# Opening of a two-block fp32 kernel: two weight units split in alternating quarters, the third block's share moved behind the third activation tile, and TensorE given small matmuls ahead of the first product

## The chip, the cores and the metric

The kernel runs on one core of one Trainium2 chip. The metric is the device time of one launch in microseconds (us). A range of 0.2% of it, some 7 us, is about what a measurement of this kernel can tell from no change.

## What is computed

Two transformer-like blocks run one behind the other on `x` of 1024 tokens by 1024 channels, all in float32. Only the opening of the first one matters here:

```python
def hybrid_layer(x, g_pre_mix, w_in, ...):
    h = rmsnorm(x, g_pre_mix)
    proj = jnp.einsum('bld,dn->bln', h, w_in)
    ...
    (u_s5, x_conv, b_conv, c_conv, q, k, v, f_logit, gate_logits) = jnp.split(proj, offsets, axis=-1)
    y_a = s5_mixer(u_s5, a_re, a_im, log_dt, b_re, b_im, c_re, c_im, d_skip, w_glu)
    y_b = short_conv_mixer(x_conv, b_conv, c_conv, conv_w)
    y_c = forgetting_attention(q, k, v, f_logit, b_f)
```

## The kernel before

**Layout.** Activations are kept transposed, channels on the 128 partitions: `x` is 8 tiles of 128 channels by 1024 tokens. A product is made block by block. A block is 128 output channels by 1024 tokens and needs one weight unit, 128 by 1024 numbers (8 squares of 128 by 128, one for each activation tile `k`), fetched from a stream in HBM in the order of use.

**Precision.** Each factor is split in a rounded high part and the rest. A product of a weight square with half an activation tile is three matmuls with 512 columns: high by high, high by low, low by high. For weights ACT casts `w_raw` to `w_hi` and POOL subtracts to get `w_lo` (`split_unit`, L276 to L284). For activations ACT writes `act_hi` (L1067), DVE writes `act_lo` (L1068). There are two slots for weight units, so a slot's next unit is fetched when its `w_lo` is done (`fetch_unit`).

**Queues.** Each engine works through its instructions in the order in which the code writes them, and waits on semaphores. An instruction that waits holds back all behind it on its engine.

**The opening** is in `s5` (the loop over `k` from L1064). The first two blocks (`first_two`, a `TwoBlocks`) and a third one (`third(k)`, weights `hi3`, `lo3`, in the trace `n1wh`, `n1wl`) are made together, tile by tile, while `x` arrives. For each `k` the order is: `act_hi`, `act_lo`, a square of `x` on ACT (`n1s`, L1073), the sum of squares on DVE (L1075), then 12 matmuls of `first_two.tile` and 6 of `third(k)`. After the tile of `k` = 0 the third unit is cast on ACT (L1084) and split on POOL (L1085); `third(0)` stands behind the tile of `k` = 1. `first_split` splits unit 0 as a whole; unit 1 is split as a whole by `first_two.tile` at its first call. Small operations of the s5 mixer (`small`, tiles `s_tm`, 128 x 16) are woven in, three steps of the generator for each `k` from 1 to 6. `squares` and their sums give the row scale `rs`, with which the blocks are evicted at the end.

**The semaphores** that the change touches: `s_whi` counts casts of units, `s_split` counts finished splits of units, and `G` (in the order listings `gpsimd`) counts marked POOL instructions. `vector` and `scalar` are the same for DVE and ACT.

Of the kernel before, what the change touches and what calls it, by code (L numbers as in the profile page):

```python
# [9 lines left out]
P = 128  # L10
L = 1024
D = 1024
KT = D // P
# [20 lines left out]
F32 = mybir.dt.float32  # L34
# [93 lines left out]
def _build(nc, ctx, t, out):  # L128
# [22 lines left out]
    V = Lane(nc.vector, sem("vector"), 1024)  # L151
# [141 lines left out]
    def first_split():  # L293

        split_unit(0, 0, 1)
        fetch_unit(2, 0)
# [116 lines left out]
    class TwoBlocks:  # L413
# [3 lines left out]
        def __init__(self, tiles, rhs, split=False, final=False, called=False):  # L417
            self.tiles, self.rhs, self.split, self.final, self.called = tiles, rhs, split, final, called
            self.base, self.begun = used["units"], False
            self.pairs = [(used["blocks"] + o) % 2 for o in range(2)]  # L420
            self.ready = {}
            advance(2, 2)

        def tile(self, o, h, k):
# [4 lines left out]
            if not self.begun:  # L429
                self.begun = True  # L430
                if not self.split and not self.called:
                    split_unit(b + 1, 1 - slot, (b + 1) // 2 + 1, 4 if b else 1)
                if not self.final:
                    fetch_unit(b + 3, 1 - slot)
            if k == 0 and h == 0:
                nc.tensor.wait_ge(s_split, b + 3)
                nc.tensor.wait_ge(reads.sem, reads.n)
# [501 lines left out]
    def s5(first_two, first_evicts, w, stored):  # L939
# [3 lines left out]
        with ExitStack() as keep:  # L943
# [103 lines left out]
            with ExitStack() as at:  # L1047
# [17 lines left out]
                for k in range(KT):  # L1065
                    g = col("g_pre_mix", k)
                    a = A.mark(A.after(arrived[k]).activation(act_hi[:, k, :], x[:, k, :], ACT.Copy, scale=g))  # L1067
                    split = V.mark(V.after(a).scalar_tensor_tensor(act_lo[:, k, :], x[:, k, :], g,  # L1068
                                                                   act_hi[:, k, :].bitcast(F32), ALU.mult, ALU.subtract))
                    if k == 0:  # L1070
                        first_split()
# [11 lines left out]
                    if k == 0:  # L1083
# [5 lines left out]
                    if k == 1:  # L1089
                        PE.after(third_ready)  # L1090
                        third(0)
                    if k == KT - 1:
                        for h in range(2):
                            spread = half_spread(h, bank[h][:], roots[h])
                            rs_ready = A.mark(A.after(spread).copy(rs[:, halves[h]], bank[h][:]))
                    if k:
                        last = third(k)
# [929 lines left out]
    with ExitStack() as at:  # L2027
# [45 lines left out]
        first_two = TwoBlocks(KT, act_rhs)  # L2073
# [172 lines left out]
```

## Time and profile before

| | before |
|---|---|
| median of 3 runs | 3443.64 us (3442.82 to 3444.27) |
| the profiled execution, its time | 3441.3 us |
| its span in the profile | 3439.6 us |
| mean granted TensorE clock | 0.996 of full speed |
| PE / DVE / ACT / POOL busy | 98% / 38% / 27% / 27% |

The span runs from the first to the last instruction; the time of the execution has 1.7 us around it. Busy shares are shares of the span. "PE" is the matmul part of TensorE, "PEld" its weight loads, which overlap it. All times in the rows are counted from the start of the span.

### The profile page before, as it was taken

How to read it: one execution, taken by the hardware profiler on the slowest of the kernel's cores; microseconds unless marked ns; L12 is line 12 of the kernel's file. 1: busy time of each engine (PE TensorE's matmuls, PEld its weight loads, DVE VectorE, ACT ScalarE, POOL GpSimd, SP SyncE). 2: the span in 40 equal slices, each digit the busy share in tenths (PEclk: the TensorE clock that was granted, in tenths of full speed). 3: DMA queues.
4: the chain of work that ended last, by engine and by line, in shares of the span. 5: the costliest groups of instructions: out<-in, count | busy, mean ns of one | idle time of the engine just before them, and what ended most of it. 6: DMA issues, size and time to landing. Idle time of an engine off the chain costs nothing.

```text
span 3439.6 us, 40933 instructions
## 1 busy us (share of the span) xinstructions
PE 3358.9 (98%) x16184; PEld 2736.7 (80%) x16184; DVE 1312.0 (38%) x1631; ACT 944.6 (27%) x1248; POOL 944.5 (27%) x507
## 2 busy tenths in 40 slices
PE   8999999999999999999999999999999999999997
PEld 6788888777877888888867777777788788888886
DVE  7852455434234131313153427555461521121123
ACT  3213444444232111111133432312352411111112
POOL 2212222213432222222321124232264222222125
PEclk9999999999999999999999999999999999999998
DMA  3535444235412111111234223214362211111113
GB/s 130 160 95 160 132 152 149 96 110 188 149 56 73 49 49 49 43 54 43 98 120 124 96 89 114 74 68 149 135 220 98 85 45 54 43 49 50 48 55 129
DMA packets 101603, 333.43 MB, mean 97 GB/s; under 512 B 11920, under 2 KB 21520, under 8 KB 101328
## 3 DMA queue, kind: packets, MB, share of 16 engines
q1 hardware_dynamic: 100432, 327.95, 28.4%
q10 hardware_dynamic: 1040, 3.67, 0.3%
q8 instruction: 90, 1.47, 0.2%
q14 instruction: 41, 0.34, 0.0%
HBM read 249.06 MB, written 85.52 MB: 97 GB/s over the span
## 4 chain that ended last, share of the span: by engine, by line
PE 86%; DVE 7%; issue 2%; DMA 2%; ACT 2%; POOL 1%; SPq 0%; DVEq 0%; ACTq 0%; POOLq 0%
PE pair L322 73%; PE pair L441 4%; PE wide L832 2%; PE bank L652 2%; PE bank L800 1%; DMA m2g<-proj 1%; PE wide L565 1%; DVE act_lo L555 1%; DVE s_tmp L958 1%; DVE hg_t L1500 1%; POOL w_lo L282 0%; DVE p L623 0%; DVE hg_pt L1519 0%; PE bank L495 0%; PE bank L473 0%
## 5 line engine op out<-in xcount | busy, mean ns | idle before, releaser
L282 POOL TENSOR_TENSOR w_lo<-w_raw,w_hi 128x1024 fp32r<-128x1024 f32 (+1 forms) x304 | 699.4, 2304 | 2337.2 <-ACT w_hi L278 2288.4
L322 PE MATMUL pair<-act_hi,w_hi 128*128 128x512 f32 x2976 | 942.0, 398 | 2.2 <-DVE p L2045 1.2
L322 PE MATMUL pair<-act_lo,w_hi 128*128 128x512 f32 x2976 | 920.0, 390 | 0.0
L322 PE MATMUL pair<-act_hi,w_lo 128*128 128x512 f32 x2976 | 918.7, 390 | 0.0
L322 PEld LDWEIGHTS pair<-act_lo,w_hi 128*128 128x128 f32 x2976 | 559.2, 188 | 119.3
L322 PEld LDWEIGHTS pair<-act_hi,w_lo 128*128 128x128 f32 x2976 | 558.9, 188 | 119.5
L322 PEld LDWEIGHTS pair<-act_hi,w_hi 128*128 128x128 f32 x2976 | 539.7, 188 | 107.0 <-issue 8.2
L278 ACT CAST w_hi<-w_raw 128x1024 fp32r<-128x1024 f32 x274 | 287.4, 1049 | 836.9 <-PE pair L322 801.0
L623 DVE TENSOR_TENSOR p<-pair,rs 128x1024 f32<-128x1024 f32 x100 | 122.2, 1222 | 403.9 <-PE pair L322 403.8
L1960 DVE TENSOR_TENSOR f2v<-pair,rs 128x1024 f32<-128x1024 f32 x42 | 51.4, 1224 | 330.7 <-PE pair L322 330.7
L322 PE MATMUL pair<-f1hh,w_lo 128*128 128x512 f32 x480 | 147.8, 389 | 0.0
L322 PE MATMUL pair<-f1hh,w_hi 128*128 128x512 f32 x480 | 147.8, 389 | 0.0
L322 PE MATMUL pair<-f1hl,w_hi 128*128 128x512 f32 x480 | 147.7, 389 | 0.0
L441 PE MATMUL pair<-act_hi,w_hi 128*128 128x512 f32 x192 | 86.4, 450 | 24.9 <-DVE act_lo L555 13.0
L1954 DVE TENSOR_TENSOR f1v<-pair,rs 128x1024 f32<-128x1024 f32 x30 | 36.7, 1225 | 183.7 <-PE pair L322 183.7
L1949 ACT CAST f1hh<-f1v 128x1024 f32 x30 | 31.5, 1050 | 273.6 <-DVE f1v L1955 273.6
L322 PEld LDWEIGHTS pair<-f1hh,w_hi 128*128 128x128 f32 x480 | 90.1, 188 | 18.7
L322 PEld LDWEIGHTS pair<-f1hh,w_lo 128*128 128x128 f32 x480 | 90.1, 188 | 18.7
L322 PEld LDWEIGHTS pair<-f1hl,w_hi 128*128 128x128 f32 x480 | 90.1, 188 | 18.7
L1986 DVE TENSOR_TENSOR f1y<-f1y,pair 128x1024 f32 x22 | 26.9, 1221 | 201.3 <-PE pair L322 201.3
L322 PE MATMUL pair<-f2hh,w_lo 128*128 128x512 f32 x328 | 101.0, 389 | 0.0
L322 PE MATMUL pair<-f2hh,w_hi 128*128 128x512 f32 x328 | 101.0, 389 | 0.0
(492 smaller groups left out, 4038.5 us busy)
## 6 DMA issues: line engine op xcount, KB each, us to landing
w_raw<-in_stream SPq DMA_DIRECT2D x275, 512.0 KB, 3.5
proj<-p SPq DMA_DIRECT2D x101, 512.0 KB, 2.6
m2g<-proj SPq DMA_DIRECT2D x32, 512.0 KB, 5.8
m1g<-proj SPq DMA_DIRECT2D x16, 512.0 KB, 3.6
x<-f1y SPq DMA_DIRECT2D x16, 512.0 KB, 2.6
act_lo<-x SPq DMA_DIRECT2D x16, 512.0 KB, 6.9
foxx<-proj SPq DMA_DIRECT2D x28, 256.0 KB, 5.8
fx_cb<-fox_cum SPq DMA_DIRECT2D x8, 512.0 KB, 7.3
```

What stands on the lines that cost most here:

```text
L278: nc.scalar.copy(whi[:, slot, :], raw[:, slot, :]).then_inc(s_whi, 1)
L282: last = nc.gpsimd.tensor_tensor(wlo[:, slot, at:at + n], raw[:, slot, at:at + n], whi[:, slot, at:at + n].bitcast(F32), ALU.subtract)
L322: last = nc.tensor.matmul(out_pair[:, h * HALF:(h + 1) * HALF], wt, a[:, h * HALF:(h + 1) * HALF], start=k == 0 and n_pass == 0, stop=k == ...
L441: last = nc.tensor.matmul(out, wt, a[:, half], start=k == 0 and n_pass == 0, stop=k == self.tiles - 1 and n_pass == 2)
L555: split[h, k] = V.mark(V.after(a).scalar_tensor_tensor(act_lo[:, k, half], yk, g, act_hi[:, k, half].bitcast(F32), ALU.mult, ALU.subtract))
L565: done[h].append(PE.mark(nc.tensor.matmul(sides[h], ones[:], sq(h, k % 2), start=k == 0, stop=k == KT - 1)))
L623: done = read(V.after(ready, stored).tensor_tensor(buf[:, slot, :], psum[:], rs[:], ALU.mult))
L652: last = nc.tensor.transpose(dst_j, src(j0 + j), ident[:])
L800: last = nc.tensor.matmul(bank[1][mine, n % 4 * P:(n % 4 + 1) * P], vt[:, k0 // P + j, mine], p[:, j, :], start=j == 0, stop=j == nk - 1)
L832: last = nc.tensor.matmul(wide[:, c:e], q[:, h % 2, q0:q0 + P], ks[:, h % 2, k0 + c:k0 + e], start=q is qh, stop=q is ql)
L1954: a = read(V.then(ready).tensor_tensor(x[:, s, :], psum[:], rs[:], ALU.mult))
L1960: v = read(V.then(ready).tensor_tensor(x[:, o, :], psum[:], rs[:], ALU.mult))
```

## The change

Four things are done. (1) `first_split` casts both first units one behind the other and subtracts them in eight pieces of 256 columns, by turns, each with its own mark; `first_two.tile` waits for the piece that it needs instead of a whole unit, and doesn't split unit 1 itself. (2) ACT and DVE make the second activation tile (`scaled(1)`) directly behind the two casts, ahead of both squares and of the third unit's cast. (3) The third unit's cast and split stand behind the tile of `k` = 1, and `third(0)` and `third(1)` stand behind the tile of `k` = 2. (4) TensorE gets 14 matmuls of `ones` by `ones`, 128 x 128 in float32, as soon as `ones` is written; their output in `bank[1]` is used by nobody.

```diff
--- before.py
+++ after.py
@@ -290,9 +290,21 @@
 
     for n in range(2):
         fetch_unit(n, n)
-    def first_split():
-
-        split_unit(0, 0, 1)
+    def first_split(pieces):
+
+        for b in range(2):
+            nc.scalar.wait_ge(s_raw[b], 16)
+            nc.scalar.wait_ge(s_mm, b + 1)
+            nc.scalar.copy(whi[:, b, :], raw[:, b, :]).then_inc(s_whi, 1)
+        for b, n in ((0, 0), (0, 1), (1, 0), (0, 2), (1, 1), (0, 3), (1, 2), (1, 3)):
+            if n == 0:
+                nc.gpsimd.wait_ge(s_whi, b + 3)
+            two = slice(2 * n * P, 2 * (n + 1) * P)
+            low = nc.gpsimd.tensor_tensor(wlo[:, b, two], raw[:, b, two], whi[:, b, two].bitcast(F32), ALU.subtract)
+            if n < 3:
+                pieces[b, 2 * n] = G.mark(low)
+            else:
+                low.then_inc(s_split, 1)
         fetch_unit(2, 0)
 
     def products(i, base, per_turn, n_out, tiles, rhs, evict, ahead=False):
@@ -414,8 +426,9 @@
 
 
 
-        def __init__(self, tiles, rhs, split=False, final=False, called=False):
+        def __init__(self, tiles, rhs, split=False, final=False, called=False, pieces=None):
             self.tiles, self.rhs, self.split, self.final, self.called = tiles, rhs, split, final, called
+            self.pieces = pieces
             self.base, self.begun = used["units"], False
             self.pairs = [(used["blocks"] + o) % 2 for o in range(2)]
             self.ready = {}
@@ -428,12 +441,15 @@
             reads, out = pair_read[self.pairs[o]], pair[self.pairs[o]][:, half]
             if not self.begun:
                 self.begun = True
-                if not self.split and not self.called:
+                if not self.split and not self.called and self.pieces is None:
                     split_unit(b + 1, 1 - slot, (b + 1) // 2 + 1, 4 if b else 1)
                 if not self.final:
                     fetch_unit(b + 3, 1 - slot)
+            if self.pieces and h == 0:
+                PE.after(self.pieces.get((b, k)))
+            if h == 0 and k == (KT - 2 if self.pieces else 0):
+                nc.tensor.wait_ge(s_split, b + 3)
             if k == 0 and h == 0:
-                nc.tensor.wait_ge(s_split, b + 3)
                 nc.tensor.wait_ge(reads.sem, reads.n)
             hi, lo = self.rhs(o, k)
             w_hi, w_lo = (x[:, slot, k * P:(k + 1) * P] for x in (whi, wlo))
@@ -1062,13 +1078,23 @@
                                                     start=k == 0 and n_pass == 0, stop=k == KT - 1 and n_pass == 2)
                     return last
 
-                for k in range(KT):
+                def scaled(k):
+
                     g = col("g_pre_mix", k)
                     a = A.mark(A.after(arrived[k]).activation(act_hi[:, k, :], x[:, k, :], ACT.Copy, scale=g))
-                    split = V.mark(V.after(a).scalar_tensor_tensor(act_lo[:, k, :], x[:, k, :], g,
-                                                                   act_hi[:, k, :].bitcast(F32), ALU.mult, ALU.subtract))
+                    return V.mark(V.after(a).scalar_tensor_tensor(act_lo[:, k, :], x[:, k, :], g,
+                                                                  act_hi[:, k, :].bitcast(F32), ALU.mult, ALU.subtract))
+
+                PE.after(ones_ready)
+                for _ in range(14):
+                    nc.tensor.matmul(bank[1][:, 0:P], ones[:], ones[:], start=True, stop=True)
+                for k in range(KT):
                     if k == 0:
-                        first_split()
+                        split = scaled(0)
+                        first_split(first_two.pieces)
+                        second = scaled(1)
+                    else:
+                        split = scaled(k) if k > 1 else second
                     sq_k = sq[:, 1 + k % 2, :] if k else squares
                     a = A.mark(A.after(added.get(k - 2)).activation(sq_k, x[:, k, :], ACT.Square))
                     if k:
@@ -1080,20 +1106,21 @@
                     for o in range(2):
                         for h in range(2):
                             first_two.tile(o, h, k)
-                    if k == 0:
+                    if k == 1:
                         a = A.mark(A.after(raw3_in).copy(hi3[:], raw3[:]))
                         third_ready = G.mark(G.after(a).tensor_tensor(lo3[:], raw3[:], hi3[:].bitcast(F32), ALU.subtract))
                         for n in range(3):
                             s5_in.mark(SP.dma_start((bb[:, 0:2, :, :], cc[:], dg[:])[n], (t["s5_b"], t["s5_c"], t["s5_d"])[n]))
                         got = s5_in.last()
-                    if k == 1:
+                    if k == 2:
                         PE.after(third_ready)
                         third(0)
+                        third(1)
                     if k == KT - 1:
                         for h in range(2):
                             spread = half_spread(h, bank[h][:], roots[h])
                             rs_ready = A.mark(A.after(spread).copy(rs[:, halves[h]], bank[h][:]))
-                    if k:
+                    if k > 1:
                         last = third(k)
                     if 0 < k < KT - 1:
                         for _ in range(3):
@@ -2070,7 +2097,7 @@
             SP.wait_ge(*v)
             return store.mark(SP.dma_start(s5_u.rearrange("(n p) j m -> n p (j m)", p=P)[1], staged))
 
-        first_two = TwoBlocks(KT, act_rhs)
+        first_two = TwoBlocks(KT, act_rhs, pieces={})
         with Woven(products(0, used["units"], n, n, KT, act_rhs, evict), n * KT, 1) as w:
             s5(first_two, (evict_row, evict_u_half, evict_third), w, stored)
             w.upto(14 * KT + 1)
```

Lines of the changed kernel have other numbers: L441 becomes L457, L1061 L1077, L1067 L1084, L1068 L1085, L1073 L1099, L1075 L1101, L1084 L1110, L1085 L1111, L958 L974, L962 L978, L966 L982, L963 L979.

**POOL, the weight splits of the opening.** In the kernel before, from `ones` on (`w_lo` are the units 0, 1 and then 2, `n1wl` is the third block's):

```order
L261 MEMSET ones 128x128 [waits gpsimd]
L282 TENSOR_TENSOR w_lo<-w_raw,w_hi 128x1024 [waits whi] x2
L1085 TENSOR_TENSOR n1wl<-n1wr,n1wh 128x1024 [waits scalar]
L282 TENSOR_TENSOR w_lo<-w_raw,w_hi 128x256 [waits whi]
L282 TENSOR_TENSOR w_lo<-w_raw,w_hi 128x256 x3
```

In the changed kernel, the same stretch:

```order
L261 MEMSET ones 128x128 [waits gpsimd]
L303 TENSOR_TENSOR w_lo<-w_raw,w_hi 128x256 [waits whi]
L303 TENSOR_TENSOR w_lo<-w_raw,w_hi 128x256
L303 TENSOR_TENSOR w_lo<-w_raw,w_hi 128x256 [waits whi]
L303 TENSOR_TENSOR w_lo<-w_raw,w_hi 128x256 x5
L1111 TENSOR_TENSOR n1wl<-n1wr,n1wh 128x1024 [waits scalar]
```

Two subtractions of 1024 columns have become eight of 256; the third unit's is still one of 1024, and still behind them.

**ACT, from the first activation tile to the third.** Before (`s_tm` are the small operations of the s5 mixer):

```order
L1067 ACTIVATE act_hi<-n1x,vec 128x1024 [waits load]
L278 CAST w_hi<-w_raw 128x1024 [waits mm,raw0]
L1073 ACTIVATE n1s<-n1x 128x1024
L278 CAST w_hi<-w_raw 128x1024 [waits mm,raw1]
L1084 CAST n1wh<-n1wr 128x1024 [waits store]
L1067 ACTIVATE act_hi<-n1x,vec 128x1024 [waits x_in1]
L1073 ACTIVATE n1s<-n1x 128x1024
L987 ACTIVATE s_tm<-vec 128x16 [waits vector]
L990 ACTIVATE s_tm<-s_tm 128x16 [waits vector]
L991 ACTIVATE s_tm<-s_tm 128x16 [waits scalar]
L1067 ACTIVATE act_hi<-n1x,vec 128x1024 [waits x_in2]
```

After:

```order
L1084 ACTIVATE act_hi<-n1x,vec 128x1024 [waits load]
L298 CAST w_hi<-w_raw 128x1024 [waits mm,raw0]
L298 CAST w_hi<-w_raw 128x1024 [waits mm,raw1]
L1084 ACTIVATE act_hi<-n1x,vec 128x1024 [waits x_in1]
L1099 ACTIVATE n1s<-n1x 128x1024 x2
L1110 CAST n1wh<-n1wr 128x1024 [waits store]
L1003 ACTIVATE s_tm<-vec 128x16 [waits vector]
L1006 ACTIVATE s_tm<-s_tm 128x16 [waits vector]
L1007 ACTIVATE s_tm<-s_tm 128x16 [waits scalar]
L1084 ACTIVATE act_hi<-n1x,vec 128x1024 [waits x_in2]
```

The second `act_hi` has moved ahead of the first square and of `n1wh`; the third `act_hi` still stands behind all of them. DVE's own order is the same in both kernels: two `act_lo`, the first sum, nine small operations, the third `act_lo`.

**PE, from the end of the tile of `k` = 1 to that of `k` = 2.** Before (`pair` are the first two blocks, `wide` is the third; twelve `wide` matmuls stand in a row):

```order
L441 MATMUL pair<-act_hi,w_lo 128x512
L1061 MATMUL wide<-act_hi,n1wh 128x512 [waits gpsimd]
L1061 MATMUL wide<-act_lo,n1wh 128x512
L1061 MATMUL wide<-act_hi,n1wl 128x512
...
L441 MATMUL pair<-act_hi,w_hi 128x512 [waits vector]
```

After:

```order
L457 MATMUL pair<-act_hi,w_lo 128x512
L457 MATMUL pair<-act_hi,w_hi 128x512 [waits gpsimd,vector]
...
L457 MATMUL pair<-act_hi,w_lo 128x512
L1077 MATMUL wide<-act_hi,n1wh 128x512 [waits gpsimd]
...
L457 MATMUL pair<-act_hi,w_hi 128x512 [waits vector]
```

The twelve `wide` matmuls that stood between the tiles of `k` = 1 and `k` = 2 now stand behind the latter, with the six of `third(2)`.

## Rows read from the trace of the kernel before

**Rows 1.** The page: shares of the chain that ended last.
```profile
PE 86%; DVE 7%; issue 2%; DMA 2%; ACT 2%; POOL 1%; SPq 0%; DVEq 0%; ACTq 0%; POOLq 0%
```

**Rows 2.** Timeline of PE: start us, us, instruction [idle before <-releaser].
```profile
11.00 0.77 PE L441 MATMUL pair<-act_hi,w_hi 128*128 128x512 f32 x1 [11.00 <-POOL w_lo L282]
...
13.70 0.63 PE L441 MATMUL pair<-act_hi,w_hi 128*128 128x512 f32 x1
...
16.56 0.50 PE L441 MATMUL pair<-act_hi,w_hi 128*128 128x512 f32 x1 [0.86 <-DVE act_lo L1068]
...
22.13 0.39 PE L441 MATMUL pair<-act_hi,w_hi 128*128 128x512 f32 x1
...
26.21 0.46 PE L441 MATMUL pair<-act_hi,w_hi 128*128 128x512 f32 x1
```

**Rows 3.** Timeline of ACT, the start.
```profile
8.94 1.03 ACT L278 CAST w_hi<-w_raw 128x1024 fp32r<-128x1024 f32 x1
...
12.26 1.15 ACT L1067 ACTIVATE act_hi<-n1x,vec 128x1024 fp32r<-128x1024 f32 x1
13.31 1.04 ACT L1073 ACTIVATE n1s<-n1x 128x1024 f32<-128x1024 f32 x1
...
18.83 1.13 ACT L1067 ACTIVATE act_hi<-n1x,vec 128x1024 fp32r<-128x1024 f32 x1
```

**Rows 4.** Timeline of DVE, the start.
```profile
7.25 1.28 DVE L1068 SCALAR_TENSOR_TENSOR act_lo<-n1x,vec,act_hi 128x1024 fp32r<-128x1024 f32 x1 [7.25 <-ACT act_hi L1067]
13.44 3.06 DVE L1068 SCALAR_TENSOR_TENSOR act_lo<-n1x,vec,act_hi 128x1024 fp32r<-128x1024 f32 x1 [4.90 <-ACT act_hi L1067]
16.54 1.22 DVE L1075 TENSOR_TENSOR n1s<-n1s 128x1024 f32<-128x1024 f32 x1
17.79 0.17 DVE L962 TENSOR_SCALAR s_tm<-vec 128x16 f32<-128x16 f32 x1
...
19.30 0.60 DVE L966 SCALAR_TENSOR_TENSOR s_tm<-s_tm 128x16 f32<-128x16 f32 x3
...
20.01 1.28 DVE L1068 SCALAR_TENSOR_TENSOR act_lo<-n1x,vec,act_hi 128x1024 fp32r<-128x1024 f32 x1
```

**Rows 5.** Timeline of POOL, the start.
```profile
2.38 0.20 POOL L261 MEMSET ones<- 128x128 f32 x1
8.16 4.92 POOL L282 TENSOR_TENSOR w_lo<-w_raw,w_hi 128x1024 fp32r<-128x1024 f32 x2 [5.58 <-ACT w_hi L278]
13.05 2.37 POOL L1085 TENSOR_TENSOR n1wl<-n1wr,n1wh 128x1024 fp32r<-128x1024 f32 x1
47.19 2.80 POOL L282 TENSOR_TENSOR w_lo<-w_raw,w_hi 128x256 fp32r<-128x256 f32 x4 [31.78 <-ACT w_hi L278]
```

**Rows 6.** Timelines of POOL and DVE from 1004: four quarters beside DVE work.
```profile
1004.49 4.10 POOL L282 TENSOR_TENSOR w_lo<-w_raw,w_hi 128x256 fp32r<-128x256 f32 x4 [1.39 <-ACT w_hi L278]
...
1004.96 1.22 DVE L555 SCALAR_TENSOR_TENSOR act_lo<-f1y,vec,act_hi 128x512 fp32r<-128x512 f32 x1
```

**Rows 7.** Timeline at 226: a small DVE operation beside POOL.
```profile
226.25 2.38 POOL L282 TENSOR_TENSOR w_lo<-w_raw,w_hi 128x1024 fp32r<-128x1024 f32 x1 [12.24 <-ACT w_hi L278]
226.41 2.31 DVE L639 TENSOR_TENSOR s_tmp<-s_tmp 128x64 f32<-128x64 f32 x1
```

**Rows 8.** DMA issues under way from 1.7 to 1.8 us, last: us to landing.
```profile
n1x<-in_x ACTq DMA_DIRECT2D x1, 512.0 KB, 6.7
w_raw<-in_stream SPq DMA_DIRECT2D x1, 512.0 KB, 7.1
```

**Rows 9.** Busy us of PE, PEld, DVE, ACT, POOL by stretch; then PEclk, DMA, GB/s.
```profile
1809.30:1812.70 3.40, 0.06 (x1) 0.00 (x0) 2.35 (x2) 3.38 (x4) 0.85 (x1) 1.00 0.03 11
...
1813.50:1816.90 3.40, 3.40 (x10) 2.66 (x9) 3.40 (x3) 0.00 (x0) 1.53 (x1) 0.50 0.00 0
```

**Rows 10.** Timeline of PE at 88 us, after a shorter idle time.
```profile
88.28 0.66 PE L652 MATMUL bank<-ident,s_state 128*128 128x128 f32 x4 [2.65 <-DVE s_state L958]
```

**Rows 11.** The chain that ended last, 0 to 110 us: two half_spread calls.
```profile
47.35 1.80 PE bank L495 x16
```

## The prediction

> **What bounds the kernel now.** I read the page first: 86% of the chain that ended last are matmuls of PE [rows 1]. Time is gained or lost here only by making PE start or stop at another moment, and the change touches only the opening. So the rest was read as a block that moves as a whole. Then I read the timelines of the four engines there. On PE [rows 2] the reader is to see three things. The first matmul waits for `w_lo` until 11.00. The first six take until 13.70, 0.45 us each, where the 18 from 22.13 to 26.21 take 4.08, 0.227 each: a slow beginning. And PE sits idle once, 0.86 us before 16.56, for the second `act_lo`. From 16.56 to 26.21 there are 42 matmuls at 0.23, so nothing more is lost. From 26.21 on (`k` = 3) the same matmuls remain in both kernels. **The question is only when `k` = 3 can start.**
>
> On DVE [rows 4] the second `act_lo` took 3.06 us, a later one 1.28. It was asked for at 13.44, while POOL's `n1wl` ran from 13.05 to 15.42 [rows 5], and ended 1.08 us behind that. At 226 us even an operation with 64 columns took 2.31 us, for as long as POOL was at a split of 1024 columns [rows 7]. DVE does not start on two SBUF inputs while POOL subtracts. I take this as the rule of the sum: the one that comes second waits for the other's whole instruction. The Trainium skill says the same ("SBUF — State Buffer", SBUF: two separate sides): the port pair that both share is an exclusive lock held for the whole instruction, not a split of bandwidth. It speaks against this change, which puts more DVE work into POOL's busy stretch; both rows of it agree, with 3.06 and 2.31 us. Without the rule the sum would be that of rival 1 (3441.9), with it the one below.
>
> **The start of PE.** Quarter (0,0) can start at 8.16 as before [rows 5]. The first `act_lo` holds DVE until 8.53 [rows 4]; four quarters alone take 2.80, 0.70 each [rows 5], so the piece ends about 9.1. Before, the whole first split ended near 13.08 - 2.37 = 10.7 (8.16 + 4.92 = 13.08 for both, 2.37 for one alone) and PE started 0.3 later. PE now starts at about 9.4, 1.6 earlier.
>
> **The 14 small matmuls.** Two `half_spread` calls, 8 float32 matmuls of this shape, take 1.80 us [rows 11], 0.225 each; at half the clock 0.45. They start when `ones` is done (2.58) and last 3.2 to 6.3 us, to 5.8 to 8.9. That ends before 9.4, so they delay nothing. If they bring the clock up, the first 12 matmuls take 0.23 instead of 0.43 to 0.45. The Trainium skill ("TensorE: Matmul & The Clock Gate", Why this matters for your kernels) tells to keep TensorE busy and to warm it up. By that rule, 1.7 us less at the front (8 cold matmuls at 0.2) would be 1.7 less in all, and with the 1.6 of the earlier start 3443.6 - 3.3 = 3440.3. From the rows I count nothing for either, since the next two waits cover both.
>
> **The wait for the second tile.** The second `w_raw`, issued at 1.7 to 1.8, lands 7.1 later [rows 8], so its cast stays near 8.85 to 9.9 [rows 3]. The second `x` tile has landed by then (at most 1.8 + 6.7 = 8.5), and the third, next on its queue, some 2.5 later. The second `act_hi` follows the cast, 9.8 to 10.95 (1.15 long, before 12.26 to 13.41). POOL is meanwhile at (1,0) from 9.95, (0,2) from 10.65 to 11.35. DVE waits for that piece and ends 1.1 later: `act_lo` is ready at 12.45, four us earlier than 16.50. PE has finished `k` = 0 by 12.3 (the block-1 half of it waits for (1,0), 10.95) and works on `k` = 1 from 12.5 to 15.2, or to 17.6 if its clock is low.
>
> **The wait for the third tile, where the gain goes.** ACT goes on with two squares (1.04 each) and the third unit's cast, 10.85 to 13.8. POOL and DVE take turns. Rows for this: beside DVE work four quarters took 4.10 instead of 2.80, and a 512-wide DVE operation 1.22 [rows 6]. In turns: (1,1) ends 13.0; the sum of squares asked at 12.85 (1.22 long) ends 14.05; (0,3) ends 14.65; the small chain starts at 14.1 instead of 17.79. Before, the third `act_hi` began 18.83 - 17.79 = 1.04 after it [rows 3, 4]; now 15.15, ended 16.3. (1,2) ends 15.35, (1,3) 16.05. Then `n1wl`, whose cast has long been done, takes POOL from 16.0 to 18.4. DVE has three small two-input operations left at that moment (0.60 for three), and behind them the third `act_lo`, which has its input from 16.3 on. They wait until 18.4, then 0.5 for the small ones, 0.2 for the one behind, 1.28 for `act_lo`: it ends at **20.35**, against 20.01 + 1.28 = 21.29 before. So it is only 0.9 earlier.
>
> Before, PE had the 12 matmuls of `third(0)` and `third(1)` to do during this wait, and reached `k` = 2 at 22.13 without a pause. Now they stand behind `k` = 2. PE is done at 15.2, idle for some 5 us, and begins `k` = 2 at 20.4. Then come 12 + 18 matmuls before `k` = 3: 30 x 0.227 = 6.8, so `k` = 3 starts at 27.2 instead of 26.21, **1.0 us later**. DVE's fourth `act_lo` ended before 26.21, at most 4.9 behind the third; now it is there by 25.3 and not the bound.
>
> **The clock behind that pause.** Behind a stretch of 3.40 us in which PE was busy for 0.06, the granted clock was 0.50 (1.2 GHz) from 1813.50 to 1816.90, with 10 matmuls in 3.40 us [rows 9]. After 2.65 us idle at 88.28 [rows 10] it was not seen to fall. Five us is past both. While the clock is at half, each matmul costs 0.2 more. A stretch like that of rows 9 overlaps the 30 matmuls wholly (8 matmuls, 1.6 us) or in part, or two in a row (up to 3.2). Bounds 0 and 3.2; I take 1.6, since the pause is longer than the one in the row.
>
> **What is hidden.** The fetches of units 2 and 3 are issued some 3 us later, since `s_split` counts whole units; all `x` tiles are queued ahead of them, and the s5 constants behind them on SP are used long after. The longer POOL stretch ends by 18.4 and its next work is at 47.19 [rows 5]. The sum of squares, the roots and the evictions follow PE.
>
> **Sum.** +1.0 + 1.6 = +2.6 us. The profiled execution (3441.3 us, 1.7 above its span) would be 3443.9; the runs shown have their median 2.3 above that execution, so 3443.64 + 2.6 = **3446.2**, which is no change by the 0.2% (6.9 us) that a measurement here can tell.
>
> **Rivals.**
> 1. *`n1wl` does not get in before the third `act_lo`* (pieces slower, or small operations not held up). Against it: it needs DVE to be some 0.9 us ahead of my turns, since `act_lo` could start at 16.95 at best and `n1wl` is due at 16.0. Then `act_lo` ends at 18.2 or earlier and `k` = 2 starts 2.1 us sooner: 27.2 - 2.1 = 25.1, a gain of 1.1; the pause is 3 us and may leave the clock up. Time 3442.5. If DVE and POOL didn't hinder each other at all, 17.6 and 3441.9. The end of this line is PE without any pause, `k` = 2 at 15.2: 22.0, 3439.4.
> 2. *The pause comes, but the clock stays.* +1.0: 3444.6. Against it rows 9; it is the lower part of my own case.
> 3. *Slower by over 0.2%.* One mechanism: the clock stays at half for longer after the pause. Each matmul costs 0.2, so beyond the +1.0 it takes 5.9 / 0.2 = 30 matmuls, all those up to `k` = 3, to decide it. Against it: in rows 9 it was 0.50 for 3.4 us while PE was fed without a break, as it would be here. With 35 it would be 3451.6.
> 4. *The small matmuls don't raise the clock,* or it falls again before 9.4. Then `k` = 0 ends near 14.5 and `k` = 1 near 17.6 to 19.6, still before 20.35: no change of the forecast, though in rival 1 it would take back up to its gain.
>
> **How the numbers follow.** My case, `k` = 3 between 26.3 and 31 (rival 2 in it): 0.78, its own range 3443.8 to 3448.5. Rival 1: 0.15. Rival 3: 0.04. 0.03 is left for a gain over 6.9 us, for which the opening has no room (PE starting at 9.4 without a pause gives 4.2) and which would have to come from elsewhere. The range takes in most of rival 1 and the two bounds of the clock: 3441.0 to 3449.0. Within 0.2% falls all but rival 3 and the rest: faster 0.03, same 0.93, slower 0.04.
>
> **What would show it.** In the changed trace: first product at 9.4; the second `act_lo` ending near 12.5 with POOL's pieces around it; `k` = 2 preceded by an idle time of PE of 4 to 5.5 us, released by `act_lo` L1085; that `act_lo` ending 1.9 to 2.2 us behind `n1wl`; the granted clock at 0.50 soon after 18; `k` = 3 at 28.8, give or take 1.5. I am wrong if the third `act_lo` runs before `n1wl`, if DVE's small operations run beside POOL, or if some stretch far behind the opening changes by more than a us on its own.

## The result and the profile after

| | before | changed |
|---|---|---|
| median, 20 runs each | 3443.57 us (3439.87 to 3447.74) | 3448.41 us (3445.38 to 3451.88) |
| ratio changed / before, 95% interval | | 1.0014 [1.0008, 1.0020] |
| profiled execution: time / span | 3441.3 / 3439.6 us | 3446.68 / 3445.0 us |
| mean granted TensorE clock | 0.996 | 0.994 |

The changed kernel is 4.8 us slower, 0.14%: less than the 0.2% that was called no change, but its interval leaves out 1. The profiled executions stand 5.4 us apart. The mean clocks are to be read with care: in the kernel before PEclk stands at 1.00 from 11.0 to 14.6, though the matmuls there come every 0.43 us, so the slow start is not in its mean.

PE's timeline of the changed kernel, to be laid beside [rows 2]:

```profile
2.74 5.62 PE L1090 MATMUL bank<-ones 128*128 128x128 f32 x28 [2.74 <-POOL ones L261]
9.31 0.47 PE L457 MATMUL pair<-act_hi,w_hi 128*128 128x512 f32 x1 [0.96 <-DVE act_lo L1085]
...
12.50 0.50 PE L457 MATMUL pair<-act_hi,w_hi 128*128 128x512 f32 x1
...
15.13 0.39 PE L457 MATMUL pair<-act_hi,w_lo 128*128 128x512 f32 x1
20.95 0.79 PE L457 MATMUL pair<-act_hi,w_hi 128*128 128x512 f32 x1 [5.43 <-DVE act_lo L1085]
21.54 0.63 PE L457 MATMUL pair<-act_lo,w_hi 128*128 128x512 f32 x1
...
24.53 0.41 PE L457 MATMUL pair<-act_hi,w_lo 128*128 128x512 f32 x1
24.77 0.40 PE L457 MATMUL pair<-act_hi,w_hi 128*128 128x512 f32 x1
...
29.54 0.39 PE L457 MATMUL pair<-act_hi,w_hi 128*128 128x512 f32 x1
```

The first product starts at 9.31 instead of 11.00, `k` = 1 at 12.50 instead of 16.56. All of that is gone at the next step. PE is done with `k` = 1 at 15.5 and then idle for 5.43 us, until the third `act_lo`. The twelve `wide` matmuls that filled this time before stand behind. And where `k` = 2 begins, matmuls come every 0.43 us; from 24.53 on every 0.23. `k` = 3 starts at 29.54 instead of 26.21: **3.3 us late.**

The same moment on POOL and DVE, beside [rows 4, 5], and ACT, beside [rows 3]:

```profile
8.24 7.86 POOL L303 TENSOR_TENSOR w_lo<-w_raw,w_hi 128x256 fp32r<-128x256 f32 x8 [5.65 <-ACT w_hi L298]
16.07 2.34 POOL L1111 TENSOR_TENSOR n1wl<-n1wr,n1wh 128x1024 fp32r<-128x1024 f32 x1
```

```profile
10.94 1.51 DVE L1085 SCALAR_TENSOR_TENSOR act_lo<-n1x,vec,act_hi 128x1024 fp32r<-128x1024 f32 x1 [2.32 <-ACT act_hi L1084]
12.91 1.23 DVE L1101 TENSOR_TENSOR n1s<-n1s 128x1024 f32<-128x1024 f32 x1 [0.46 <-ACT n1s L1099]
14.17 0.59 DVE L978 TENSOR_SCALAR s_tm<-vec 128x16 f32<-128x16 f32 x1
15.04 0.42 DVE L974 TENSOR_TENSOR s_tm<-s_tm 128x16 f32<-128x16 f32 x1 [0.28 <-ACT s_tm L1003]
15.50 0.65 DVE L974 TENSOR_TENSOR s_tm<-vec,s_tm 128x16 f32<-128x16 f32 x1
16.18 2.69 DVE L978 TENSOR_SCALAR s_tm<-s_tm 128x16 f32<-128x16 f32 x3
18.90 0.59 DVE L982 SCALAR_TENSOR_TENSOR s_tm<-s_tm 128x16 f32<-128x16 f32 x3
19.53 0.17 DVE L979 TENSOR_SCALAR s_tm<-s_tm 128x16 f32<-128x16 f32 x1
19.62 1.28 DVE L1085 SCALAR_TENSOR_TENSOR act_lo<-n1x,vec,act_hi 128x1024 fp32r<-128x1024 f32 x1
```

```profile
8.81 1.05 ACT L298 CAST w_hi<-w_raw 128x1024 fp32r<-128x1024 f32 x1 [0.65 <-DMA w_raw<-in_stream]
9.76 1.15 ACT L1084 ACTIVATE act_hi<-n1x,vec 128x1024 fp32r<-128x1024 f32 x1
...
15.87 1.13 ACT L1084 ACTIVATE act_hi<-n1x,vec 128x1024 fp32r<-128x1024 f32 x1
```

The reader is to see who holds whom. The second `act_lo` is 1.51 long instead of 3.06 and ends at 12.45: the part of the change that does what it says. The sum of squares behind it gets its turn at once (1.23) and it is a POOL piece that waits. The three small operations behind that wait for the POOL piece in progress; one of 16 columns takes 0.42 to 0.65. At 16.07 `n1wl` takes POOL until 18.41. The three `TENSOR_SCALAR` that start at 16.18 last 2.69 together, because the first is held for all of `n1wl` (three of them took 0.59 at 18.67 in the trace before). The third `act_hi` has been there since 17.0. Its `act_lo` stands in DVE's queue behind seven small operations and starts at 19.62, to end at 20.90.

The busy time by stretches (columns: length; busy of PE, PEld, DVE, ACT, POOL; PEclk; DMA share; GB/s):

```profile
15.50:17.70 2.20, 0.02 (x1) 0.00 (x0) 2.17 (x2) 2.17 (x4) 2.20 (x2) 1.00 1.02 417
17.71:20.94 3.23, 0.00 (x0) 0.00 (x0) 2.99 (x9) 1.52 (x2) 0.71 (x1) 0.50 0.92 335
20.95:24.53 3.58, 3.58 (x9) 2.81 (x10) 2.61 (x10) 2.07 (x5) 0.00 (x0) 0.50 0.03 13
24.54:29.50 4.96, 4.96 (x23) 4.13 (x22) 4.79 (x7) 4.96 (x6) 0.00 (x0) 1.00 0.01 3
...
92.81:99.63 6.82, 6.05 (x21) 4.59 (x20) 6.79 (x4) 2.10 (x3) 4.53 (x1) 0.50 0.30 97
```

The granted clock is 0.50 (1.2 GHz) from 17.7 to 24.5, that is over the second half of the pause and the first eight matmuls of `k` = 2. A second low stretch of 6.8 us lies at 92.8, 1.3 us behind a pause of 2.67 that the kernel before has too [rows 10]. Follow one matmul through it, first in the changed kernel, then in the kernel before:

```profile
91.50 0.66 PE L668 MATMUL bank<-ident,s_state 128*128 128x128 f32 x4 [2.67 <-DVE s_state L974]
...
102.57 0.63 PE L668 MATMUL bank<-ident,s_state 128*128 128x128 f32 x4 [0.77 <-ACT s_first L672]
```

```profile
96.58 0.63 PE L652 MATMUL bank<-ident,s_state 128*128 128x128 f32 x4 [0.77 <-ACT s_first L656]
```

The pause at 88 us ends 3.22 us later than before (91.50 against 88.28). At the matmul behind the low stretch it is 5.99 (102.57 against 96.58). Near the end it is 5.4:

```profile
3429.93 2.08 PE L511 MATMUL bank<-ident,tok 128*128 128x128 f32 x8 [4.13 <-DVE tok L509]
```

Before, this one stands at 3424.54. So the 5.4 us of the profiles are 3.2 from the opening, 2.8 from the clock at 92.8, and -0.6 over the rest. In the opening, 1.5 us are the order (20.95 + 30 x 0.227 = 27.76 against 26.21) and 1.8 the clock (29.54 - 27.76). At full clock e2, below, took 6.98 for these 30 matmuls, since the first of them is longer; counted so, it is 1.7 and 1.6.

### The profile page after: what moved, and what is told of

It reads as the page before. It is cut to its first block, busy times and chain, and to the rows that moved or that the text cites. A ratio compares the mean times of both kernels' runs of the same rounds, so it can differ in the third digit from the quotient of the medians.

```text
span 3445.0 us, 40998 instructions
## 1 busy us (share of the span) xinstructions
PE 3366.4 (98%) x16212; PEld 2744.2 (80%) x16212; DVE 1313.7 (38%) x1631; ACT 945.1 (27%) x1248; POOL 946.8 (27%) x513
## 3 DMA queue, kind: packets, MB, share of 16 engines
q1 hardware_dynamic: 100432, 327.95, 28.4%
## 4 chain that ended last, share of the span: by engine, by line
PE 88%; DVE 7%; issue 2%; ACT 1%; DMA 1%; POOL 0%; SPq 0%; DVEq 0%; ACTq 0%; POOLq 0%
PE pair L334 75%; PE pair L457 4%; PE wide L848 2%; PE bank L668 2%; PE bank L816 1%; PE wide L581 1%; DVE act_lo L571 1%; DVE s_tmp L974 1%; DVE hg_t L1527 1%; DVE p L639 0%; DVE hg_pt L1546 0%; PE bank L511 0%; PE bank L489 0%; DVE f1y L555 0%; DVE s_state L974 0%
## 5 line engine op out<-in xcount | busy, mean ns | idle before, releaser
L457 PE MATMUL pair<-act_hi,w_hi 128*128 128x512 f32 x192 | 86.3, 450 | 19.7 <-DVE act_lo L571 13.1
```

Source lines behind the costliest of these rows:

```text
L457: last = nc.tensor.matmul(out, wt, a[:, half], start=k == 0 and n_pass == 0, stop=k == self.tiles - 1 and n_pass == 2)
```

## The experiments

Medians of 11 runs; each group has its own runs of the kernel before beside it. The intervals of the ratios are about 0.0009 to each side, 3 us. So **the opening is read from the profiles, the medians only bear it out**. Where the first products start also differs by some 0.5 us between executions of like programs, with the landing of the first tiles.

| run | first product | `k` = 2 | `k` = 3 | `k` = 4 | median | before beside it |
|---|---|---|---|---|---|---|
| before | 11.00 | 22.13 | 26.21 | 30.39 | | 3443.57 |
| changed | 9.31 | 20.95 | 29.54 | 33.62 | 3448.41 | 3443.57 |
| e1_no_small | 9.86 | 22.27 | 32.08 | 36.16 | 3445.89 | 3443.51 |
| e2_filled_pause | 9.38 | 21.91 | 28.89 | 32.97 | 3447.17 | 3443.51 |
| e3_third_behind | 9.69 | 19.21 | 27.75 | 31.82 | 3445.75 | 3443.51 |
| e4_n1wl_quarters | 9.39 | 21.39 | 29.81 | 33.89 | 3448.78 | 3443.51 |
| e8_thirds_ahead | 9.49 | 23.93 | 28.48 | 32.56 | 3445.54 | 3442.58 |
| e5_small_alone | 11.11 | 22.42 | 26.50 | 30.64 | 3445.81 | 3442.58 |
| e6_chain_behind | 9.77 | 16.36 | 19.71 | 28.83 | 3442.52 | 3442.58 |
| e7_before_again | 11.12 | 22.26 | 26.34 | 30.51 | 3440.97 (one) | 3442.58 |
| e9_best_no_small | 9.46 | 17.24 | 19.96 | 28.63 | 3440.64 | 3443.82 |
| e12_best_small | 9.27 | 16.12 | 19.49 | 28.58 | 3441.99 | 3443.82 |
| e10_small_again | 11.49 | 22.77 | 26.85 | 31.05 | 3444.92 | 3443.82 |
| e11_change_again | 9.29 | 21.92 | 30.50 | 34.58 | 3450.76 | 3443.82 |

(`k` = 4 is comparable in all rows: the same 72 matmuls lie ahead of it everywhere.)

**e1_no_small: without the small matmuls.**

```diff
-                PE.after(ones_ready)
-                for _ in range(14):
-                    nc.tensor.matmul(bank[1][:, 0:P], ones[:], ones[:], start=True, stop=True)
```

> The changed kernel without its 14 small matmuls. Account A (the opening's delay comes from the third activation tile waiting behind n1wl, with PE in a pause): the first product at 9.3, the first twelve matmuls at 0.43 to 0.45 us each, k = 1 done before 18; k = 2 still starts at 20.9 +- 0.3, since its act_lo comes no earlier; time within 1.5 us of the changed kernel (3448.4). Account B (the small matmuls themselves, or the clock that they raise early, cause the loss or set when the clock falls later): k = 2 starts elsewhere, or the time goes back by 2 to 5 us towards 3443.6.

The first products were slow as expected and `k` = 1 was over at 17.9. `k` = 2 came at 22.27, not 20.95, since the whole chain ran later in this execution (the second weight unit landed later, its cast began at 10.11 instead of 8.81, and the second `act_lo` ended at 13.74, 1.3 later). The third `act_lo` ended 8.48 behind the second, in the changed kernel 8.45: the small matmuls have no part in the wait. The clock was low from 21.6 to 28.4, that is over nearly all the first matmuls of `k` = 2, so the 30 matmuls took 9.81 us, 2.8 more than at full clock. This profiled execution was the slowest of its 11 (3450.58). The median is 2.5 us under the changed kernel, outside the 1.5 that account A allowed and inside account B's 2 to 5, although the opening is no shorter; it comes up again below.

**e2_filled_pause: 22 matmuls more, into the pause.**

```diff
                     if k == 1:
+                        for _ in range(22):
+                            nc.tensor.matmul(bank[1][:, 0:P], ones[:], ones[:], start=True, stop=True)
                         a = A.mark(A.after(raw3_in).copy(hi3[:], raw3[:]))
```

> The changed kernel with 22 more small matmuls behind the tile of k = 1 (about 5 us of work that nobody uses, into the pause). Account A: k = 2 starts at 20.9 as before, the granted clock stays 1.00 there, and k = 3 starts at 20.9 + 30 x 0.227 = 27.7 instead of 29.5; time 1.8 us (1.6 to 2.6) under the changed kernel, 3446.6, still 1.5 to 3 over before. Account B (the clock has nothing to do with the pause): half the clock near 18 to 24 all the same, k = 3 at 29.5, time as the changed kernel.

Its PE timeline:

```profile
21.91 0.50 PE L457 MATMUL pair<-act_hi,w_hi 128*128 128x512 f32 x1 [0.53 <-DVE act_lo L1085]
...
28.89 0.39 PE L457 MATMUL pair<-act_hi,w_hi 128*128 128x512 f32 x1
```

From `k` = 2 to `k` = 3 it took 6.98 us instead of 8.59, 30 matmuls at 0.23, with the granted clock at 1.00 throughout. So the clock behind the pause costs 1.6 us, and the pause is its cause. The other profiles bear that out: in all six with a pause of 2.93 us or more before the third tile (changed, e1, e3, e4, e8, e11) the clock fell in it or within 0.4 us behind it, in none of the four where PE waited 0.53 us or less there (e2, e6, e9, e12). `k` = 3 came at 28.89 and not at 27.7, since `k` = 2 came 1.0 later here (the second unit's cast began at 9.76). The median is 1.2 us under the changed kernel, less than the 1.6 to 2.6 expected, which intervals of 3 us can't tell apart.

**e3_third_behind: the third unit's cast and split behind the third `act_lo`.**

```diff
-                    if k == 1:
+                    if k == 2:
                         a = A.mark(A.after(raw3_in).copy(hi3[:], raw3[:]))
-                        third_ready = G.mark(G.after(a).tensor_tensor(lo3[:], raw3[:], hi3[:].bitcast(F32), ALU.subtract))
+                        third_ready = G.mark(G.after(a, split).tensor_tensor(lo3[:], raw3[:], hi3[:].bitcast(F32), ALU.subtract))
+                    if k == 1:
```

> The changed kernel with the third unit's cast and split moved behind the act_lo of k = 2, nothing else. Account A: POOL is free from 16.1, the nine small DVE operations end by 17.1, act_lo of k = 2 ends at 18.3 instead of 20.9, k = 2 starts at 18.4, n1wl ends at 21.5 and third(0) waits some 0.3 us for it; k = 3 starts at 25.5 to 26 if the clock stays (pause 3.0 us), up to 27.5 if it falls; time 3442.9 to 3445, clearly under the changed kernel. Account B (DVE isn't held by the lock but by its own chain of small operations with ACT): act_lo of k = 2 still ends at 20 or later, time as the changed kernel.

The third `act_lo` now ends 6.34 us behind the second instead of 8.45, at 19.16. So `n1wl`'s place ahead of it cost 2.1 us. `k` = 3 stands at 27.75, just past the upper end: the pause was 3.32, the clock was low for a part of `k` = 2, and `k` = 2 itself came 0.8 later than expected. The median, 3445.75, missed its range (3442.9 to 3445) too.

**e4_n1wl_quarters: `n1wl` in four pieces.**

```diff
-                        third_ready = G.mark(G.after(a).tensor_tensor(lo3[:], raw3[:], hi3[:].bitcast(F32), ALU.subtract))
+                        G.after(a)
+                        for q in range(4):
+                            two = slice(2 * q * P, 2 * (q + 1) * P)
+                            low = nc.gpsimd.tensor_tensor(lo3[:, two], raw3[:, two], hi3[:, two].bitcast(F32), ALU.subtract)
+                        third_ready = G.mark(low)
```

> The changed kernel with n1wl made in four pieces of 256 columns, nothing else. Account A (exclusive, held for one instruction at a time): DVE's operations get in between the pieces; the first small one waits 0.6 us instead of 2.2, act_lo of k = 2 ends at 19.3 to 19.9 instead of 20.9, n1wl ends 1 to 2 us later than 18.4, k = 2 starts at 19.4 to 20; time 1 to 2 us under the changed kernel. If POOL keeps the lock over its pieces: act_lo at 20.9, time as the changed kernel.

The turns were as account A says, the times were not: it had the third `act_lo` at 19.3 to 19.9 and a gain of 1 to 2 us. POOL, then DVE in this stretch:

```profile
16.73 2.76 POOL L1114 TENSOR_TENSOR n1wl<-n1wr,n1wh 128x256 fp32r<-128x256 f32 x4
```

```profile
16.83 2.02 DVE L978 TENSOR_SCALAR s_tm<-s_tm 128x16 f32<-128x16 f32 x3
18.88 1.06 DVE L982 SCALAR_TENSOR_TENSOR s_tm<-s_tm 128x16 f32<-128x16 f32 x3
...
20.06 1.28 DVE L1085 SCALAR_TENSOR_TENSOR act_lo<-n1x,vec,act_hi 128x1024 fp32r<-128x1024 f32 x1
```

DVE does get in between the pieces, so the lock is held for one instruction. But each small operation buys only itself that place and the next one waits for the next quarter: three took 2.02 us, 0.65 each. Four of the seven small ones paid for a quarter, which is as long as one wait for the whole. The third `act_lo` ended 8.24 behind the second (at 21.34), 0.2 better than with `n1wl` whole, and the median stayed at the changed kernel's.

**e8_thirds_ahead: `third(0)` and `third(1)` in front of `k` = 2 again.**

```diff
-                    if k == 2:
+                    if k == 1:
                         PE.after(third_ready)
                         third(0)
-                        third(1)
...
-                    if k > 1:
+                    if k:
                         last = third(k)
```

> The changed kernel with third(0) and third(1) ahead of the tile of k = 2 again, as in the kernel before. Account A: PE pauses from 15.4 to n1wl's end, about 18.7, does the twelve matmuls until 21.4 and goes on with k = 2 at once; k = 3 at 25.5 if the clock stays, up to 27.3 if it falls in the pause of 3.2 us; 2 to 4 us under the changed kernel, -1 to +1 against the kernel before. If the moved matmuls aren't what made the pause dear, it stays near the changed kernel (k = 3 at 29).

```profile
18.64 0.80 PE L1077 MATMUL wide<-act_hi,n1wh 128*128 128x512 f32 x1 [2.93 <-POOL n1wl L1111]
...
23.93 0.63 PE L457 MATMUL pair<-act_hi,w_hi 128*128 128x512 f32 x1
...
28.48 0.39 PE L457 MATMUL pair<-act_hi,w_hi 128*128 128x512 f32 x1
```

`third(0)` starts behind `n1wl`, after 2.93 us idle, and the twelve matmuls run while `act_lo` is made: `k` = 3 comes 1.1 earlier than in the changed kernel (28.48). It missed the expected 25.5 to 27.3, since the clock was low from 18.0 to 24.9 and `third(0)`, `third(1)` took 5.3 us instead of 2.7. The pause is 2.50 us shorter than in the changed kernel (2.93 against 5.43), the 30 matmuls behind it took 1.25 longer (9.84 against 8.59), because more of them fell into the low clock, and this execution began 0.18 later: that leaves the 1.1. The median is 2.9 us under the changed kernel, as expected, but 3.0 over the kernel before, where -1 to +1 was expected.

**e5_small_alone and e10_small_again: the kernel before with the 14 small matmuls.**

```diff
+                PE.after(ones_ready)
+                for _ in range(14):
+                    nc.tensor.matmul(bank[1][:, 0:P], ones[:], ones[:], start=True, stop=True)
                 for k in range(KT):
                     g = col("g_pre_mix", k)
```

> The kernel before with the 14 small matmuls alone. Account A (they win nothing, since the second act_lo is waited for anyway): the first product at 11.0 as before, the first twelve matmuls at 0.23 us instead of 0.43, k = 1 at 16.6 and k = 3 at 26.2 as before, time within 1 us of the kernel before. By the page's rule (the clock won at the front passes through): 1.7 us under it.

> The kernel before with the 14 small matmuls alone, a second time. Account A (its 3.2 us over the kernel before in the first comparison were chance: low stretches of the clock that fall where they fall): median within 1.5 us of the kernel before, k = 3 at 26.2 to 26.5. Account C (they cost something systematic): again 2 to 3.5 us over it.

Two stretches of the first one, columns as above:

```profile
11.20:14.50 3.30, 3.30 (x8) 2.62 (x9) 0.68 (x1) 2.81 (x3) 3.30 (x2) 0.50 1.03 420
...
89.70:96.40 6.70, 5.93 (x19) 4.39 (x18) 6.67 (x4) 2.24 (x4) 4.54 (x1) 0.50 0.25 101
```

In the opening both did as the kernel before (`k` = 3 at 26.50 and 26.85, each 15.4 us behind its first product, before 15.2). But the first matmuls were not faster: the small ones end at 8.5, 2.64 us ahead of the first product at 11.1, and the granted clock was 0.50 from there to 14.5 (in the second one to 17.1). A warm-up that ended 2.64 and 3.42 us early won nothing. The low stretch at 89.7 is also here, in a kernel whose work there is unchanged.

The medians were 3.2 and 1.1 us over the kernel before. Two more pairs differ in the small matmuls alone: changed against e1_no_small (+2.5) and e12_best_small against e9_best_no_small (+1.35). The signs agree, and no single ratio to the kernel before stands out of its interval. Taken by means and together they do: the four differences of the means are 2.7, 2.0, 2.1 and 1.6, with standard errors of 0.7 to 0.9, and their average is 2.1 with one of 0.4. (The changed kernel and e1 come from two comparisons.)

The profiles show where such a time would lie. It is not in the opening, it is in stretches of low clock behind it:

| low clock between `k` = 4 and 3410 us, in all | executions | from `k` = 4 to the end of the span |
|---|---|---|
| about 10 us | before, e7, e9 | 3408.4 to 3409.2 us |
| about 14 us | e2, e3, e6 | 3411.7 to 3412.0 us |
| about 17 us | changed, e8 | 3411.4 and 3412.9 us |
| about 20 us | e1, e4, e5, e10, e11, e12 | 3412.2 to 3415.8 us |

All ten executions with small matmuls ahead stand in the lower three rows; of the four without them three are in the first row and one, e1, is in the last. If the small matmuls had no part in it, the three shortest would all be executions without them about once in 90 times (4 of 364). The comparison was made after the fact, with one execution for most kernels, and no run shows how matmuls that end before 9 us could bring low stretches hundreds of us later. It is likely, not shown.

**e7_before_again and e11_change_again: both kernels unchanged.**

> The kernel before, unchanged, one look for a second profile of it. Account A: k = 3 starts at 26.2 give or take 0.5; the granted clock may fall at other places than in the first profile (at 92 us behind the pause of 2.65, at 799), since the same program shows its low stretches at places that differ from execution to execution.

> The changed kernel, unchanged, again. Account A: k = 3 at 28.5 to 31, depending on where the low stretch lies in the pause; 3 to 4 us over the kernel before from the opening, the rest of the first comparison's 4.8 chance: median 2.5 to 5 over it. If the stretch 84 to 100 us of the first profile (18.7 us instead of 15.9) belongs to the change, it is there again.

The kernel before gave the same opening, without a low stretch near 92. The changed kernel showed `k` = 3 at 30.50 (the second `act_lo` ended 1.0 later than in the first profile) with the clock low from 18.6 to 25.4 and again from 93.7 to 100.5. Its median is 6.9 us over the kernel before, where 2.5 to 5 was expected; the profiled execution was the slowest of its 11. Over 14 profiles of all these kernels, the pause of 2.65 to 2.69 us near 88 was followed by a low stretch in nine, not in the two of the kernel before, e1, e2 and e3. Near 800, where the code is the same too, nine of the 14 had one.

**e6_chain_behind, then e9 and e12: what stood ahead of the third `act_lo` moved away.**

```diff
-                    if k == 1:
+                    if k == 3:
                         a = A.mark(A.after(raw3_in).copy(hi3[:], raw3[:]))
-                        third_ready = G.mark(G.after(a).tensor_tensor(lo3[:], raw3[:], hi3[:].bitcast(F32), ALU.subtract))
+                        third_ready = G.mark(G.after(a, split).tensor_tensor(lo3[:], raw3[:], hi3[:].bitcast(F32), ALU.subtract))
+                    if k == 1:
...
-                    if k == 2:
+                    if k == 3:
                         PE.after(third_ready)
-                        third(0)
-                        third(1)
+                        for j in range(3):
+                            third(j)
...
-                    if k > 1:
+                    if k > 2:
                         last = third(k)
-                    if 0 < k < KT - 1:
-                        for _ in range(3):
+                    if 2 < k < KT - 1:
+                        for _ in range(5 if k < 5 else 4):
```

> The changed kernel with both things that stood ahead of the third act_lo moved: the s5 mixer's small operations begin only behind the tile of k = 3 (5, 5, 4, 4 steps), and the third unit's cast and split stand behind the act_lo of k = 3, with third(0) to third(3) behind that tile. Account A: act_lo of k = 2 ends at 16.5 (with the eight pieces by turns), k = 2 starts at 16.6 with a pause of 1.0 us, k = 3 behind it without one, third(0) at about 22.2, k = 4 at 27.6 to 28.5 instead of 30.4 before and 33.6 in the changed kernel; clock 1.00 throughout; time 2 to 3 us under the kernel before, 3441. If something else holds PE up in the opening, k = 4 starts at 30 or later.

> The run with both moved behind the tile of k = 3, without the 14 small matmuls, and with 3, 5, 5, 5 steps of the s5 mixer's small operations at k = 3 to 6 (they held the act_lo of k = 4 up to 28.7). Account A (only the opening differs, and the small matmuls are neutral there, because k = 4 waits for n1wl and act_lo): k = 4 at 28.4 to 29 instead of 30.4 before; time 1.5 to 2 us under the kernel before. Account C (small matmuls ahead of the first product cost some 2 us somewhere far behind the opening): this kernel is 2 us or more under the same with them.

> The same with the 14 small matmuls. Account A: as without them, within 1 us; k = 4 at 28.6. Account C: 2 us more than without them, level with the kernel before.

e9 and e12 have `range(3 if k == 3 else 5)` in the last line, and e9 no small matmuls. PE's timeline of e9:

```profile
9.46 0.76 PE L457 MATMUL pair<-act_hi,w_hi 128*128 128x512 f32 x1 [9.46 <-POOL w_lo L303]
...
14.48 0.40 PE L457 MATMUL pair<-act_hi,w_hi 128*128 128x512 f32 x1
...
17.24 0.39 PE L457 MATMUL pair<-act_hi,w_hi 128*128 128x512 f32 x1
...
19.96 0.39 PE L457 MATMUL pair<-act_hi,w_hi 128*128 128x512 f32 x1
...
23.01 0.50 PE L1077 MATMUL wide<-act_hi,n1wh 128*128 128x512 f32 x1 [0.17 <-POOL n1wl L1108]
...
28.63 0.39 PE L457 MATMUL pair<-act_hi,w_hi 128*128 128x512 f32 x1
```

The first twelve matmuls are slow (0.42 each; this kernel leaves the small matmuls out). From 14.48 on the tiles follow one another without a pause over 0.4 us, the clock stays up, and `k` = 4 starts at 28.63: 1.8 us ahead of the kernel before and 5.0 ahead of the changed one. e6 and e12 show the same at 28.83 and 28.58. In e6 the third `act_lo` ends 3.37 us behind the second, against 6.34 in e3 and 8.45 in the changed kernel: of the 5.1 us that stood ahead of it the small operations with their turns were 3.0, `n1wl` 2.1.

The medians follow only in part. e6's, 3442.52, is level with the kernel before beside it (3442.58), though 2 to 3 us less was expected, and its `k` = 4 lies a little past the expected 27.6 to 28.5. e12's is 1.8 us under the kernel before and 1.35 over e9's; account A had allowed 1 us between the two, account C had asked for 2. e9's median, 3440.64, is the lowest of all: 3.2 under the kernel before (0.9994 [0.9985, 1.0003]) and 7.8 under the changed one. Against the changed kernel that is clear; against the kernel before the opening is shown, the time only likely.

## Why the prediction held, point by point

- **Start of PE** (predicted 9.4): 9.31. **Second `act_lo`** (12.45): 12.45. **The pieces by turns** ending at 16.05 with `n1wl` to 18.4: 16.1 and 18.41. The last two rest on one rule, that DVE and POOL take turns by whole instructions. It held in the opening of every run.
- **Third `act_lo`** (20.35): 20.90. I had taken `TENSOR_SCALAR`, which has one SBUF input, to pass beside POOL. It does not: 16 columns took 0.59 at 14.17 and the first of the three at 16.18 waited for all of `n1wl`. So the chain ahead of `act_hi` took 0.7 more than counted: 0.4 by that first operation, and 0.2 by the `TENSOR_TENSOR` at 15.04 (0.42 instead of 0.18), which has two inputs and which my own rule would have held up; I had left its turn out. Seven small operations were left behind `n1wl` instead of four. Only this cost anything, 0.55 us: `act_hi` was ready at 17.0, well before its `act_lo` could start. The Trainium skill ("SBUF — State Buffer", SBUF: two separate sides) names DVE operations in a 2-port mode beside those with two inputs as contending. The rows here agree with that and not with my narrower use of it; in which mode this `TENSOR_SCALAR` ran, no trace here shows.
- **The pause and the order term** (5 us idle, `k` = 3 later by 1.0): 5.43 idle, and 1.5. The step that was too small is the one above.
- **The clock term** (1.6, bounds 0 and 3.2): 1.6 to 1.8 in the profile, and 1.6 by filling the pause (e2). That the middle of the bounds came out is luck in part: where more of the low stretch lay over the matmuls, in e1 and e8, the 30 matmuls took 2.8 and 2.9 us more than at full clock.
- **Opening in all** (+2.6, `k` = 3 at 28.8): +3.3, 29.54. Right in its mechanism, short by 0.7.
- **The rest as a block that moves as a whole**: this part was wrong of the profiles, by the prediction's own sign (a stretch far behind the opening that changes by more than a us on its own). Another 2.8 us came from a low clock at 92.8, and the median of 20 runs moved by 4.8, 1.5 more than the opening. The cause is open. The work there is unchanged and the low stretch comes and goes with the execution, which speaks for chance in a profile; chance should average out over 20 runs, and the second comparison of the changed kernel gave +6.9. The four pairs put some 2 us on the small matmuls, and the profiles with them have more low clock behind the opening, but no run shows how the one would bring the other.
- **The time** (3446.2, range 3441.0 to 3449.0): 3448.41, 0.6 under the upper end. The +2.6 of the sum stands against +4.8, and the second comparison's +6.9 would have been outside. So the range held with some luck; what it left out is the point above.
- **A slip without effect**: by the prediction's own turns piece (1,0) ended at 10.65, not at 10.95.
- **Rival 1** (`act_lo` before `n1wl`) did not happen on its own; e3 made it happen by order, for 2.1 us. **Rival 4** (the small matmuls don't raise the clock) did not happen, they did: 0.23 each from the first product on. e1, where the first products are slow, shows what it says of the sum: the wait for the third `act_lo` is the same. **The warm-up rule of the Trainium skill** ("TensorE: Matmul & The Clock Gate", Why this matters for your kernels), as the prediction applied it, gave 3440.3 for this change (with 1.7 for 8 matmuls at 0.2, which is 1.6); the rows gave nothing for it. In the changed kernel the warm-up did work and PE then stood still for 5.43 us, so nothing of it was left; in the old order (e5) it ended 2.64 us before there was work, and the second `act_lo` would have been waited for in any case.

## What to carry to other kernels

An early tile is worth what stands behind it: ask which operation will be waited for next, and what is queued ahead of it on its engine, down to the smallest operation. Cutting one engine's long instruction into pieces lets the other in once for each piece; a chain of small operations pays a piece for each of its links (e4: 0.2 us won), so it is better to move the chain or the long instruction (e3 and e6: 2.1 and 5.1 us). And before moving matmuls back, ask which wait they were covering: here 12 of them (2.7 us) had filled a wait; without them PE stood still for 5.43 us, and the low clock behind that cost another 1.6 to 1.8.

## What was not expected of the hardware

- A one-input `TENSOR_SCALAR` of 16 columns waits for POOL like any other: 0.59 to 0.65 beside a 256-column piece, 2.27 beside `n1wl`, against 0.17 to 0.18 alone. In e6 one such operation stands by itself beside `n1wl`:

```profile
20.95 2.24 DVE L978 TENSOR_SCALAR s_tm<-vec 128x16 f32<-128x16 f32 x1
```

```profile
19.80 3.36 POOL L1111 TENSOR_TENSOR n1wl<-n1wr,n1wh 128x1024 fp32r<-128x1024 f32 x1 [1.23 <-DVE act_lo L1085]
```

One with a single element in each partition passed, though: 0.15 at 312.55 in the kernel before, while POOL was at a split from 311.73 to 314.13.
- The reverse holds too: with DVE's sum ahead of it, `n1wl` took 3.33 in e3 and 3.36 in e6, 2.34 in the changed kernel.
- Of 14 executions with a 2.65 to 2.69 us pause of PE at the same place, nine had the granted clock at 0.50 soon behind it, for 3.4 to 6.8 us, at 1.3 to 2.8 us each (by the distance from the matmul behind the pause to the one followed above, 8.30 us in the kernel before). One profile can't tell whether such a stretch belongs to a kernel.
